# Last normalisation: both parameter rows in matmul banks, two blocks to ScalarE and GpSimd, two through the tensor engine one at a time

## The chip, the cores and the metric

The kernel runs on one core of one Trainium2 chip. The metric is the device time of one execution in microseconds (us), as the median of several runs. The engines are TensorE (PE in the profile), VectorE (DVE), ScalarE (ACT), GpSimd (POOL) and SyncE (SP), which here only issues transfers.

## What is computed

One encoder layer over 1024 tokens of 1024 channels in float32: a mixing sub-layer (convolution and chunked attention), then a grouped mixture of experts, each followed by a layer norm. Only the last step matters here:

```
def layer_norm(x, g, b):
    mu = mean(x); var = mean((x - mu)**2)
    return (x - mu) * rsqrt(var + 1e-5) * g + b
x = layer_norm(ALPHA * x + grouped_moe(x, ...), ln2_g, ln2_b)
```

`ln2_g` and `ln2_b` are rows of 1024 channels, the same for every token.

## The kernel before, in words

Tokens lie on the 128 partitions, in 8 blocks t = 0 to 7 of 128 tokens. The experts run over tiles of 128 gathered tokens (20 or so, the count is read at run time). Each tile's result, times its weight, is added by an indirect transfer into `acc_dram`, whose row has 1024 channels and, as its last element, their sum. The last tile isn't added there: its rows of `acc_dram` are gathered into `rows_l`, the result in the two banks ps 6 and 7 is added by VectorE (`last_rows`), and they are normalised as a ninth block (t = 8, `TT`) and scattered over the output at the very end by GpSimd, which first waits for all eight stores of the output (`f_out`).

The last stage runs over t = 0 to 8. Rows of `acc_dram` come into `xf[:, t]` (eight loads by SyncE, L1434). For each block VectorE makes the negative mean `nmr` (`mean`, L2075); ScalarE squares with that bias and sums (L1846), and takes the root (L1849); VectorE makes (x + nmr) * g (`scale_row`, L2082), then the reciprocal (L2088), and, in `finish`, times rstd plus b (L2094). For blocks 1, 3 and 5 (`ON_PE`), `finish` writes only a diagonal matrix of rstd (L2091); TensorE makes ident x b (L1730) plus diag x rows (L1734) in two banks per block, and ScalarE copies them back (L1853). ScalarE also sums `rows_l` with a copy to `norm_l` (L1844). `g2_b` and `b2_b` hold the two parameter rows on every partition in SBUF, loaded during the experts. Order within an engine is the order in the program; engines wait on semaphores: `f_nm` (mean), `f_sq` (squares), `f_sd` (root), `f_rs` (reciprocal), `f_g` (scaled), `f_ok` (finished), `tot_set` (copied back), `fin_done` (matmuls done), `ln2_in` (parameters loaded).

VectorE's loop is

```
mean(0)
for t in range(TT + 1):
    if t == TT // 2:
        last_rows()
    if t < TT:
        mean(t + 1)
    scale_row(t)
    finish(t)
```

SyncE issues the eight stores of `xf` (L1441) in the order t = 0 to 7, each after a wait for its block; a block that is late holds back those behind it.

On TensorE, ahead of this stage, the last tiles run `up_rows`, `transpose_h(end1)` (four transposes of `hb`, L1652) and `down(end1)` (24 products, L1556 to L1558, with `dn_h`, `dn_l`).

Of the kernel before, what the change touches and what calls it, by code (L numbers as in the profile page):

```python
# [83 lines left out]
def encoder_layer(nc, xT, x, wblk, b_in, dw, dwb, lncg, lncb, relb, b_o, ln1_g, ln1_b,  # L84
# [5 lines left out]
    with ctx:  # L90
# [155 lines left out]
        blk_used = sem("blk_used")  # L246
        zero_ok = sem("zero_ok"); zero_out = sem("zero_out"); init_p = sem("init_p")
        sig_ready = sem("sig_ready"); u_ready = sem("u_ready"); conv_d = sem("conv_d")
# [19 lines left out]
        ln_g = sem("ln_g"); x1_ok = sem("x1_ok")  # L268
        x1_out = sem("x1_out"); acc_out = sem("acc_out"); wr_in = sem("wr_in"); cst_in = sem("cst_in")

# [121 lines left out]
        with nc.Block() as block:  # L392
            @block.sync
            def _(sp):
# [31 lines left out]
                sp.wait_ge(zero_ok, 1)  # L426
                sp.dma_start(acc_dram[SEQ:SEQ + P, :], zeros[:]).then_inc(zero_out, 16)
                for n in range(RING, B_V[0] + RING):
# [41 lines left out]
                for t in range(TT):  # L470
                    if t == TT - 1:
                        sp.wait_ge(wo_done, 2 * TT)
                        moe_parts["load_expert_1"](sp, 0, 2)
                    sp.wait_ge(x1_ok, t + 1)
                    if t == 5:
                        sp.dma_start(upto_t[:], consts[:, C_UPTO:C_WIDTH]).then_inc(cst_in, 16)
                    sp.dma_start(x1_dram[P * t:P * t + P, :], x1[:, t, :]).then_inc(x1_out, 16)
                    sp.dma_start(acc_dram[P * t:P * t + P, 0:D], x1[:, t, :]).then_inc(acc_out, 16)
# [820 lines left out]
def moe(nc, sem, m):  # L1299
# [6 lines left out]
    (x1, x1t, hot_a, hot_b, wr_t, ones, rt_a, rt_b, rank_a, rank_b, slot_i, mh, sums, xgh2, xgl2, hot_0, both, upto_t, val, wide, tc, id0, one_i, init_p, wo_add, gu, dn_h, dn_l, dn_raw, xg, xgh, xgl, hb, hbh, hbl, ys,  # L1306
     xf, g2_b, b2_b, rows_l, norm_l, ys2, diag, squares, x1_tot, w_last, to_last, cst, eps2, st6, mv, rstd, nmr, wgt, ids_i, id_now, to_i, to_now, w_slot, tab, cum_i, ends_i, rows_i, br_b,
     ps, psf, ident) = (m[k] for k in (
         "x1 x1t hot_a hot_b wr_t ones rt_a rt_b rank_a rank_b slot_i mh sums xgh2 xgl2 hot_0 both upto_t val wide tc id0 one_i init_p wo_add gu dn_h dn_l dn_raw xg xgh xgl hb hbh hbl ys "
         "xf g2_b b2_b rows_l norm_l ys2 diag squares x1_tot w_last to_last cst eps2 st6 mv rstd nmr wgt ids_i id_now to_i to_now w_slot tab cum_i ends_i rows_i br_b "  # L1310
         "ps psf ident").split())
    wexp, ln2_g, ln2_b, out, x1_dram, acc_dram = (m[k] for k in "wexp ln2_g ln2_b out x1_dram acc_dram".split())
    row_in, wr_in, cst_in, wo_done, x1_ok, x1_out, acc_out, xres_ok = (
        m[k] for k in "row_in wr_in cst_in wo_done x1_ok x1_out acc_out xres_ok".split())
    gu_in = [sem(f"gu_in{j}") for j in range(4)]; dn_in = sem("dn_in")
# [12 lines left out]
    rows_in = sem("rows_in"); rows_ok = sem("rows_ok"); w_set = sem("w_set"); last_stored = sem("last_stored")  # L1328
    tot_set = sem("tot_set"); fin_done = sem("fin_done"); f_nm = sem("f_nm"); f_sq = sem("f_sq"); f_sd = sem("f_sd")
    f_rs = sem("f_rs"); f_g = sem("f_g"); f_ok = sem("f_ok"); f_out = sem("f_out")  # L1330
# [128 lines left out]
    def pool_part(pool):  # L1459
# [100 lines left out]
    def tensor_part(pe):  # L1560
# [145 lines left out]
        def step(i):  # L1706
# [46 lines left out]
    def scalar_part(act):  # L1753
# [178 lines left out]
    def vector_part(dve):  # L1932
# [137 lines left out]
        def mean(t):  # L2070
            if t < TT:
                dve.wait_ge(row_in[t], 32)
            else:
                dve.wait_ge(rows_ok, 2)
            dve.tensor_scalar(nmr[:, t:t + 1], xf[:, t, D:D + 1] if t < TT else mv[:, t, 0:1], -1.0 / D, None, ALU.mult).then_inc(f_nm, 1)  # L2075

        def scale_row(t):
            dve.wait_ge(f_nm, t + 1)
            if t < TT:

                dve.wait_ge(f_sq, t + 1)
            dve.scalar_tensor_tensor(out=xf[:, t, 0:D] if t < TT else norm_l[:], in0=xf[:, t, 0:D] if t < TT else rows_l[:, 0:D],  # L2082
                                     scalar=nmr[:, t:t + 1], in1=g2_b[:], op0=ALU.add, op1=ALU.mult).then_inc(f_g, 1)

        def finish(t):
            rows = xf[:, t, 0:D] if t < TT else norm_l[:]
            dve.wait_ge(f_sd, t + 1)
            dve.reciprocal(rstd[:, t:t + 1], rstd[:, t:t + 1]).then_inc(f_rs, 1)  # L2088
            dve.wait_ge(f_rs, t + 1)
# [3 lines left out]
            dve.wait_ge(f_g, t + 1)  # L2093
# [68 lines left out]
```

## Time and profile before

| | |
|---|---|
| median of 3 runs | 1140.38 us (1139.57 to 1140.88) |
| the profiled execution's own time | 1142.64 us |
| its span, first to last instruction | 1140.8 us |
| busy share of the span: PE, DVE, ACT, POOL | 96%, 70%, 46%, 21% |
| mean granted TensorE clock | 0.986 of full speed |

The span is what the trace shows; 1.8 us of the profiled execution lie around it. Times in the rows below are microseconds from the span's start. The last normalisation fills 1109 to 1134.

### The profile page before, as it was taken

The numbers are of one execution on the slowest core, as the hardware profiler recorded it, in microseconds if no ns is written. First come the engines' busy times: TensorE is split into PE (matmuls) and PEld (weight loads), VectorE is DVE, ScalarE is ACT, GpSimd is POOL, SyncE is SP. The second block draws the span as 40 slices with busy tenths as digits, with TensorE's granted clock in tenths as the row PEclk, the third lists the DMA queues.
The fourth block names the chain that finished last, engine by engine and source line by source line (L and its number), as shares of the span: only waits on it lengthen the run. The fifth ranks groups of instructions, "written<-read, shape, count | busy, mean of one in ns | idle before, by whom it ended". The sixth has DMA issues, their size and how long they took to land.

```text
span 1140.8 us, 16949 instructions
## 1 busy us (share of the span) xinstructions
PE 1098.7 (96%) x5549; PEld 912.7 (80%) x5550; DVE 801.2 (70%) x1153; ACT 528.8 (46%) x786; POOL 234.9 (21%) x191
## 2 busy tenths in 40 slices
PE   7999999999999999999999999999999999999984
PEld 5888888888978889788888887787888888888762
DVE  5699999935447765566685587797589646548767
ACT  5111111123456755646331134377578545648654
POOL 0000000000046864757100000124122111211220
PEclk9999999999999999999999998899999999999987
DMA  7121233232111010271731326589999876699966
GB/s 263 50 90 55 74 111 94 91 111 93 56 37 43 19 43 1 87 301 38 256 136 60 148 111 250 216 321 361 327 328 383 310 240 189 214 378 326 344 202 239
DMA packets 49797, 199.57 MB, mean 175 GB/s; under 512 B 7248, under 2 KB 7632, under 8 KB 47680
## 3 DMA queue, kind: packets, MB, share of 16 engines
q1 hardware_dynamic: 43536, 176.19, 41.1%
q0 software_dynamic: 6192, 22.49, 8.0%
q8 instruction: 40, 0.66, 0.3%
q14 instruction: 29, 0.24, 0.1%
HBM read 166.21 MB, written 32.52 MB: 174 GB/s over the span
## 4 chain that ended last, share of the span: by engine, by line
PE 84%; DMA 5%; DVE 5%; ACT 2%; POOL 2%; issue 2%; ACTq 0%; DVEq 0%; SPq 0%; POOLq 0%
PE ps L540 16%; PE ps L542 16%; PE ps L541 16%; PE ps L1556 9%; PE ps L1558 9%; PE ps L1557 8%; DMA gu<-in_wexp 3%; PE ps L640 2%; PE ps L626 2%; PE ps L612 2%; PE ps L1625 1%; PE ps L1552 1%; DMA dn_raw<-in_wexp 1%; PE ps L1540 1%; POOL pr L498 1%
## 5 line engine op out<-in xcount | busy, mean ns | idle before, releaser
L540 PE MATMUL ps<-xh,wh 128*128 128x512 f32 x512 | 204.5, 399 | 8.3 <-DVE xl L1024 8.0
L541 PE MATMUL ps<-xl,wh 128*128 128x512 f32 x512 | 200.6, 392 | 0.0
L542 PE MATMUL ps<-xh,wl 128*128 128x512 f32 x512 | 200.4, 391 | 0.0
L498 POOL TENSOR_SCALAR pr<-pr,rinv 128x640 f32<-128x640 f32 (+4 forms) x64 | 94.3, 1486 | 382.4 <-DVE rinv L1148 382.2
L1456 DVE TENSOR_TENSOR gu<-gu (+1 forms) x128 | 148.6, 1220 | 32.7 <-issue 22.3
L1047 DVE SCALAR_TENSOR_TENSOR cv<-u,dw_t,cv 128x1024 f32<-128x1024 f32 x120 | 154.1, 1284 | 3.7
L1450 ACT ACTIVATE gu<-gu (+1 forms) x128 | 124.4, 1048 | 27.2 <-DMA gu<-in_wexp 19.6
L1556 PE MATMUL ps<-gu,xgh 128*128 x336 | 133.2, 397 | 3.5 <-DVE xgl L1930 3.4
L1558 PE MATMUL ps<-gu,xgl 128*128 x336 | 131.2, 390 | 0.0
L1557 PE MATMUL ps<-gu,xgh 128*128 x336 | 130.8, 389 | 0.0
L540 PEld LDWEIGHTS ps<-xh,wh 128*128 128x128 f32 x512 | 96.8, 189 | 31.2 <-issue 12.0
L542 PEld LDWEIGHTS ps<-xh,wl 128*128 128x128 f32 x512 | 96.8, 189 | 20.5
L541 PEld LDWEIGHTS ps<-xl,wh 128*128 128x128 f32 x512 | 97.0, 189 | 19.5 <-issue 0.5
L856 ACT ACTIVATE wh<-raw 128x1024 fp32r<-128x1024 f32 x52 | 54.6, 1058 | 97.4 <-DMA raw<-in_wblk 97.1
L1019 DVE TENSOR_TENSOR wl<-raw,wh 128x1024 fp32r<-128x1024 f32 x39 | 47.6, 1222 | 50.1 <-ACT wh L856 50.1
L2022 DVE TENSOR_TENSOR dn_l<-dn_raw,dn_h 128x1024 fp32r<-128x1024 f32 x60 | 69.6, 1219 | 11.9 <-ACT dn_h L1773 11.0
L1556 PEld LDWEIGHTS ps<-gu,xgh 128*128 128x128 f32 x336 | 63.1, 188 | 17.2 <-issue 4.9
L1558 PEld LDWEIGHTS ps<-gu,xgl 128*128 128x128 f32 x336 | 63.1, 188 | 13.4
L1557 PEld LDWEIGHTS ps<-gu,xgh 128*128 128x128 f32 x336 | 63.2, 188 | 12.5
L1556 PE MATMUL ps<-dn_h,hbh 128*128 128x512 f32 x168 | 68.4, 407 | 1.9 <-DVE hbl L2026 1.9
L1557 PE MATMUL ps<-dn_l,hbh 128*128 128x512 f32 x168 | 66.5, 396 | 0.0
L1558 PE MATMUL ps<-dn_h,hbl 128*128 128x512 f32 x168 | 66.5, 396 | 0.0
(271 smaller groups left out, 2028.4 us busy)
## 6 DMA issues: line engine op xcount, KB each, us to landing
gu<-in_wexp SPq DMA_DIRECT2D x64, 1024.0 KB, 8.9
dn_raw<-in_wexp SPq DMA_DIRECT2D x16, 2048.0 KB
raw<-in_wblk SPq DMA_DIRECT2D x52, 512.0 KB, 4.1
gate_cols<-gst SPq DMA_DIRECT2D x16, 512.0 KB, 5.1
xf<-acc_rows SPq DMA_DIRECT2D x8, 512.5 KB, 7.9
xraw<-in_xT SPq DMA_DIRECT2D x8, 512.0 KB, 7.5
gcm<-gate_cols SPq DMA_DIRECT2D x8, 512.0 KB, 7.0
gam<-gate_cols SPq DMA_DIRECT2D x8, 512.0 KB, 15.6
```

The lines of the kernel that those rows point to most:

```text
L498: pool.tensor_scalar(pr[n % 3][:, h, 0:nt * P], pr[n % 3][:, h, 0:nt * P], rinv[:, n % 3, h:h + 1], None, ALU.mult).then_inc(p_ready, 1)
L540: pe.matmul(o, a_h, b_h, start=first, stop=False)
L541: pe.matmul(o, a_h, b_l, start=False, stop=False)
L542: return pe.matmul(o, a_l, b_h, start=False, stop=last)
L856: act.activation(hi, src, ACT.Copy).then_inc(w_hi, 1)
L1047: dve.scalar_tensor_tensor(out=cv[:, j, :], in0=tap, scalar=w, in1=cv[:, j, :], op0=ALU.mult, op1=ALU.add).then_inc(conv_d, 1)
L1450: eng.activation(gu[:, par, k, 0, :], gu[:, par, k, 1, :].bitcast(F32), ACT.Copy).then_inc(gu_hi, 1)
L1456: eng.tensor_tensor(gu[:, par, k, 1, :], gu[:, par, k, 1, :].bitcast(F32), gu[:, par, k, 0, :], ALU.subtract).then_inc(gu_lo, 1)
L1556: pe.matmul(o, a_h, b_h, start=first, stop=False)
L1557: pe.matmul(o, a_h, b_l, start=False, stop=False)
L1558: return pe.matmul(o, a_l, b_h, start=False, stop=last)
L2022: dve.tensor_tensor(dn_l[:, k, :], dn_raw[:, k, :], dn_h[:, k, :], ALU.subtract).then_inc(dn_lo, 1)
```

## The change

- `norm_rows(0)` and `norm_rows(1)` on TensorE multiply `g2_b` and `b2_b` by the identity into banks 0 and 1, and 2 and 3: before `transpose_h(end1)` and after it. VectorE waits for both after `mean(0)` and reads g and b there.
- Blocks 1 and 2 (`ON_POOL`): VectorE makes nmr * rstd (`shift`), ScalarE x * rstd + shift, GpSimd times g, then plus b.
- Blocks 3 and 5 (`ON_PE`) go through banks 4 and 5, the second after the first was copied back.
- The sum of `rows_l` comes out of `last_rows` itself, and ScalarE's copy to `norm_l` goes.
- Semaphores are merged: `zero_out` into `acc_out`, `cst_in` into `wr_in`, with the counts waited for raised.

```
@@ constants
-    ON_PE = (1, 3, 5)
-    STORED = {t: n for n, t in enumerate(t for t in range(TT + 1) if t not in ON_PE)}
+    ON_PE = (3, 5)
+    ON_POOL = (1, 2)
+    SCALED = {t: n for n, t in enumerate(t for t in range(TT + 1) if t not in ON_POOL)}
+    STORED = {t: n for n, t in enumerate(t for t in SCALED if t not in ON_PE)}
@@ SyncE, order of the stores
             if t in ON_PE:
                 sp.wait_ge(tot_set, 2 + ON_PE.index(t))
+            elif t in ON_POOL:
+                sp.wait_ge(z_done, 2 * ON_POOL.index(t) + 2)
             else:
@@ GpSimd, after the gather of rows_l
+        pool.wait_ge(ln2_in, 32)
+        for n, t in enumerate(ON_POOL):
+            pool.wait_ge(z_ok, n + 1)
+            pool.tensor_tensor(xf[:, t, 0:D], xf[:, t, 0:D], g2_b[:], ALU.mult).then_inc(z_done, 1)
+            pool.wait_ge(z_done, 2 * n + 1)
+            pool.tensor_tensor(xf[:, t, 0:D], xf[:, t, 0:D], b2_b[:], ALU.add).then_inc(z_done, 1)
         pool.wait_ge(f_ok, STORED[TT] + 1)
@@ TensorE
+        def norm_rows(n):
+            rows = (g2_b, b2_b)[n]
+            pe.wait_ge(ln2_in, 32)
+            for h in range(2):
+                last = pe.matmul(ps[:, 2 * n + h, :], ident, rows[:, HALF * h:HALF * h + HALF], start=True, stop=True)
+            last.then_inc(fin_done, 1)
+        norm_rows(0)
         transpose_h(end1)
+        norm_rows(1)
         down(end1, by_row=True)
         for n, t in enumerate(ON_PE):
-            halves_of = [(ps[:, 2 * n + h, :], slice(HALF * h, HALF * h + HALF)) for h in range(2)]
+            if n:
+                pe.wait_ge(tot_set, 1 + n)
             (ident x b, then diag x rows, now both into ps 4 and 5)
@@ ScalarE, in the loop over t, after the root
+            if t - 1 in ON_POOL:
+                n = ON_POOL.index(t - 1)
+                act.wait_ge(f_rs, t + n + 1)
+                act.activation(xf[:, t - 1, 0:D], xf[:, t - 1, 0:D], ACT.Identity, scale=rstd[:, t - 1:t],
+                               bias=shift[:, t - 1:t]).then_inc(z_ok, 1)
@@ ScalarE, before t == TT - 2
-                act.activation(norm_l[:], rows_l[:, 0:D], ACT.Copy, accum_out=mv[:, TT, 0:1]).then_inc(rows_ok, 1)
@@ VectorE
-                                     scalar=nmr[:, t:t + 1], in1=g2_b[:], op0=ALU.add, op1=ALU.mult).then_inc(f_g, 1)
+                                     scalar=nmr[:, t:t + 1], in1=psf[:, 0:D], op0=ALU.add, op1=ALU.mult).then_inc(f_g, 1)
+            if t in ON_POOL:
+                dve.tensor_scalar(shift[:, t:t + 1], nmr[:, t:t + 1], rstd[:, t:t + 1], None, ALU.mult).then_inc(f_rs, 1)
+                return
-            dve.scalar_tensor_tensor(out=rows, in0=rows, scalar=rstd[:, t:t + 1], in1=b2_b[:],
+            dve.scalar_tensor_tensor(out=rows, in0=rows, scalar=rstd[:, t:t + 1], in1=psf[:, D:2 * D],
@@ VectorE, last_rows
-                                     op0=ALU.mult, op1=ALU.add).then_inc(rows_ok, 1)
+                                     op0=ALU.mult, op1=ALU.add, accum_out=mv[:, TT, 0:1]).then_inc(rows_ok, 1)
@@ VectorE, the loop
-        dve.wait_ge(ln2_in, 32)
         mean(0)
+        dve.wait_ge(fin_done, 2)
         for t in range(TT + 1):
             if t == TT // 2:
                 last_rows()
             if t < TT:
                 mean(t + 1)
-            scale_row(t)
+            if t not in ON_POOL:
+                scale_row(t)
             finish(t)
```

## Rows read from the trace of the kernel before

**Rows 1.** The chain of waits, its end: start us, us, what

```profile
1130.27 1.30 DVE xf L2094
...
1131.59 2.62 DMA out_rows<-xf
1134.21 0.03 POOLq L1528
...
1135.14 1.02 POOL out_rows L1529
```

**Rows 2.** The timeline of VectorE: start us, us, engine, line, operation, names

```profile
1109.05 0.22 DVE L2075 TENSOR_SCALAR nmr<-xf 128x1 f32<-128x1 f32 x2
...
1119.14 1.28 DVE L2101 SCALAR_TENSOR_TENSOR rows_l<-ps,w_last,rows_l 128x1024 f32<-128x1024 f32 x1
1120.34 0.14 DVE L2075 TENSOR_SCALAR nmr<-xf 128x1 f32<-128x1 f32 x1
...
1132.67 0.16 DVE L2088 RECIPROCAL rstd<-rstd 128x1 f32<-128x1 f32 x1
1132.86 1.28 DVE L2094 SCALAR_TENSOR_TENSOR norm_l<-norm_l,rstd,b_b 128x1024 f32<-128x1024 f32 x1
```

**Rows 3.** The timeline of ScalarE in the same stage

```profile
1114.65 0.30 ACT L1849 ACTIVATE rstd<-mv,eps 128x1 f32<-128x1 f32 x1
...
1120.03 1.14 ACT L1846 ACTIVATE squares<-xf,nmr 128x1024 f32<-128x1024 f32 x1
...
1121.29 0.29 ACT L1849 ACTIVATE rstd<-mv,eps 128x1 f32<-128x1 f32 x1
1121.49 1.13 ACT L1846 ACTIVATE squares<-xf,nmr 128x1024 f32<-128x1024 f32 x1
```

**Rows 4.** Groups by shape from 1098 on: busy us, mean ns | idle before

```profile
L2082 DVE SCALAR_TENSOR_TENSOR xf<-xf,nmr,g_b 128x1024 f32<-128x1024 f32 x8 | 10.2, 1280 | 2.7 <-ACT squares L1846 2.7
...
L1844 ACT ACTIVATE norm_l<-rows_l 128x1024 f32<-128x1024 f32 x1 | 1.0, 1044 | 0.0
...
L2091 DVE TENSOR_SCALAR diag<-ident_t,rstd 128x128 f32<-128x128 f32 x3 | 0.9, 287 | 0.1
```

**Rows 5.** Groups by shape over the whole span, ScalarE and VectorE

```profile
L914 ACT ACTIVATE cv<-cv,cpar 128x1024 f32<-128x1024 f32 x4 | 4.6, 1234 | 0.0
```

```profile
L1139 DVE DVE_READ_ACCUMULATOR2_ANT nmx<- 128x1 f32 x62 | 5.1, 83 | 0.0
```

**Rows 6.** Groups by shape of GpSimd over the whole span

```profile
L504 POOL TENSOR_TENSOR wl<-raw,wh 128x1024 fp32r<-128x1024 f32 x13 | 31.2, 2397 | 6.5 <-ACT wh L856 6.5
```

**Rows 7.** The timeline of GpSimd (once ScalarE, its producer) at three places

```profile
383.56 0.20 POOL L512 MEMSET bias<- 64x128 f32 x1
383.82 0.20 POOL L514 MEMSET bias<- 64x128 f32 x1
```

```profile
464.36 1.06 ACT L953 ACTIVATE uoh<-cv 128x1024 fp32r<-128x1024 f32 x1
```

```profile
465.51 2.37 POOL L520 TENSOR_TENSOR uol<-cv,uoh 128x1024 fp32r<-128x1024 f32 x1 [0.19 <-ACT uoh L953]
```

```profile
535.97 7.13 POOL L534 TENSOR_TENSOR al<-attn,ah 128x1024 fp32r<-128x1024 f32 x3
```

**Rows 8.** The timeline of VectorE beside the last of these

```profile
539.42 0.61 DVE L1163 TENSOR_TENSOR attn<-ps,attn 64x128 f32<-64x128 f32 x2
```

**Rows 9.** SyncE's issues, and the stretches with transfers: us, busy by engine, PEclk, DMA share, GB/s

```profile
1120.16 0.81 SPq L1441 DMA_DIRECT2D out_rows<-xf  x2
```

```profile
1121.00:1122.00 1.00, 1.00 (x4) 0.46 (x3) 0.64 (x1) 0.97 (x4) 0.00 (x0) 1.00 1.03 414
1122.00:1123.00 1.00, 1.00 (x4) 0.48 (x3) 0.96 (x3) 0.97 (x4) 0.00 (x0) 1.00 0.99 401
1123.00:1124.00 1.00, 1.00 (x3) 0.19 (x1) 1.00 (x2) 1.00 (x3) 0.00 (x0) 1.00 0.59 229
```

**Rows 10.** The timeline of TensorE around the last transposes

```profile
1104.67 0.66 PE L1652 MATMUL ps<-ident_t,hb 128*128 128x128 f32 x4 [3.00 <-DVE hb L2038]
1107.19 0.79 PE L1556 MATMUL ps<-dn_h,hbh 128*128 128x512 f32 x1 [1.86 <-DVE hbl L2026]
...
1118.91 1.88 PE L1730 MATMUL ps<-b_b,ident_t 128*128 128x512 f32 x4
```

**Rows 11.** One line's instructions: the loads of xf, and VectorE's whole-row scaling

```profile
L1434 SPq DMA_DIRECT2D xf<-acc_rows x8: 326/438/592, 1104.3 to 1107.8; - x8
...
DMA to landing us min/median/max: 3.3/7.9/11.2
```

```profile
L1044 DVE TENSOR_SCALAR cv<-u,dw_t,cpar x4: 806/808/816, 39.8 to 184.6; 128x1024 f32<-128x1024 f32 x4
```

**Rows 12.** Table loads of ScalarE over the whole span, groups by shape

```profile
L1839 ACT ACT_TABLE_LOAD x1 | 1.3, 1283 | 0.0
```

More of the change, by code:

```diff
@@ L212, in encoder_layer @@
         nmr = tiny("nmr", [P, TT + 1])
+        shift = tiny("shift", [P, TT])
         wgt = tiny("wgt", [P, 2, TT])
@@ L246, in encoder_layer @@
         blk_used = sem("blk_used")
-        zero_ok = sem("zero_ok"); zero_out = sem("zero_out"); init_p = sem("init_p")
+        zero_ok = sem("zero_ok"); init_p = sem("init_p")
         sig_ready = sem("sig_ready"); u_ready = sem("u_ready"); conv_d = sem("conv_d")
@@ L268, in encoder_layer @@
         ln_g = sem("ln_g"); x1_ok = sem("x1_ok")
-        x1_out = sem("x1_out"); acc_out = sem("acc_out"); wr_in = sem("wr_in"); cst_in = sem("cst_in")
+        x1_out = sem("x1_out"); acc_out = sem("acc_out"); wr_in = sem("wr_in");
         def wait_used(eng, n):
@@ L426, in _ @@
                 sp.wait_ge(zero_ok, 1)
-                sp.dma_start(acc_dram[SEQ:SEQ + P, :], zeros[:]).then_inc(zero_out, 16)
+                sp.dma_start(acc_dram[SEQ:SEQ + P, :], zeros[:]).then_inc(acc_out, 16)
                 for n in range(RING, B_V[0] + RING):
@@ L475, in _ @@
                     if t == 5:
-                        sp.dma_start(upto_t[:], consts[:, C_UPTO:C_WIDTH]).then_inc(cst_in, 16)
+                        sp.dma_start(upto_t[:], consts[:, C_UPTO:C_WIDTH]).then_inc(wr_in, 16)
                     sp.dma_start(x1_dram[P * t:P * t + P, :], x1[:, t, :]).then_inc(x1_out, 16)
@@ L1306, in moe @@
     (x1, x1t, hot_a, hot_b, wr_t, ones, rt_a, rt_b, rank_a, rank_b, slot_i, mh, sums, xgh2, xgl2, hot_0, both, upto_t, val, wide, tc, id0, one_i, init_p, wo_add, gu, dn_h, dn_l, dn_raw, xg, xgh, xgl, hb, hbh, hbl, ys,
-     xf, g2_b, b2_b, rows_l, norm_l, ys2, diag, squares, x1_tot, w_last, to_last, cst, eps2, st6, mv, rstd, nmr, wgt, ids_i, id_now, to_i, to_now, w_slot, tab, cum_i, ends_i, rows_i, br_b,
+     xf, g2_b, b2_b, rows_l, norm_l, ys2, diag, squares, x1_tot, w_last, to_last, cst, eps2, st6, mv, rstd, nmr, shift, wgt, ids_i, id_now, to_i, to_now, w_slot, tab, cum_i, ends_i, rows_i, br_b,
      ps, psf, ident) = (m[k] for k in (
          "x1 x1t hot_a hot_b wr_t ones rt_a rt_b rank_a rank_b slot_i mh sums xgh2 xgl2 hot_0 both upto_t val wide tc id0 one_i init_p wo_add gu dn_h dn_l dn_raw xg xgh xgl hb hbh hbl ys "
-         "xf g2_b b2_b rows_l norm_l ys2 diag squares x1_tot w_last to_last cst eps2 st6 mv rstd nmr wgt ids_i id_now to_i to_now w_slot tab cum_i ends_i rows_i br_b "
+         "xf g2_b b2_b rows_l norm_l ys2 diag squares x1_tot w_last to_last cst eps2 st6 mv rstd nmr shift wgt ids_i id_now to_i to_now w_slot tab cum_i ends_i rows_i br_b "
          "ps psf ident").split())
     wexp, ln2_g, ln2_b, out, x1_dram, acc_dram = (m[k] for k in "wexp ln2_g ln2_b out x1_dram acc_dram".split())
-    row_in, wr_in, cst_in, wo_done, x1_ok, x1_out, acc_out, xres_ok = (
-        m[k] for k in "row_in wr_in cst_in wo_done x1_ok x1_out acc_out xres_ok".split())
+    row_in, wr_in, wo_done, x1_ok, x1_out, acc_out, xres_ok = (
+        m[k] for k in "row_in wr_in wo_done x1_ok x1_out acc_out xres_ok".split())
     gu_in = [sem(f"gu_in{j}") for j in range(4)]; dn_in = sem("dn_in")
@@ L1328, in moe @@
     rows_in = sem("rows_in"); rows_ok = sem("rows_ok"); w_set = sem("w_set"); last_stored = sem("last_stored")
-    tot_set = sem("tot_set"); fin_done = sem("fin_done"); f_nm = sem("f_nm"); f_sq = sem("f_sq"); f_sd = sem("f_sd")
+    tot_set = sem("tot_set"); fin_done = sem("fin_done"); z_ok = sem("z_ok"); z_done = sem("z_done"); f_nm = sem("f_nm"); f_sq = sem("f_sq"); f_sd = sem("f_sd")
     f_rs = sem("f_rs"); f_g = sem("f_g"); f_ok = sem("f_ok"); f_out = sem("f_out")
@@ L1409, in sync_part @@
         sp.wait_ge(x1_out, 16 * TT)
-        sp.wait_ge(acc_out, 16 * TT)
+        sp.wait_ge(acc_out, 16 * TT + 16)
         sp.wait_ge(xt_r, TT)
@@ L1470, in pool_part @@
         pool.wait_ge(x1_out, 16 * TT)
-        pool.wait_ge(acc_out, 16 * TT)
+        pool.wait_ge(acc_out, 16 * TT + 16)
         pool.wait_ge(xt_r, TT)
@@ L1511, in pool_part @@
         step(1, False)
-        pool.wait_ge(acc_out, 16 * TT + 16)
+        pool.wait_ge(acc_out, 16 * TT + 32)
         step(2)
@@ L1721, in tensor_part @@
         up_rows(NE - 1, bass.ds(par, 1), range(KC // 2, KC))
+        norm_rows(0)
         transpose_h(end1)
+        norm_rows(1)
         down(end1, by_row=True)
-        pe.wait_ge(ln2_in, 32)
         for n, t in enumerate(ON_PE):
-            halves_of = [(ps[:, 2 * n + h, :], slice(HALF * h, HALF * h + HALF)) for h in range(2)]
-            for o, c in halves_of:
-                pe.matmul(o, ident, b2_b[:, c], start=True, stop=False)
-            pe.wait_ge(f_g, t + 1)
+            if n:
+                pe.wait_ge(tot_set, 1 + n)
+            for h in range(2):
+                pe.matmul(ps[:, 4 + h, :], ident, b2_b[:, HALF * h:HALF * h + HALF], start=True, stop=False)
+            pe.wait_ge(f_g, SCALED[t] + 1)
             pe.wait_ge(diag_ok, n + 1)
-            for o, c in halves_of:
-                last = pe.matmul(o, diag[:, n, :], xf[:, t, c], start=False, stop=True)
+            for h in range(2):
+                last = pe.matmul(ps[:, 4 + h, :], diag[:, n, :], xf[:, t, HALF * h:HALF * h + HALF], start=False, stop=True)
             last.then_inc(fin_done, 1)
@@ L1840, in scalar_part @@
         for t in range(TT + 1):
-            if t == TT - 2:
-                act.wait_ge(rows_ok, 1)
-                act.activation(norm_l[:], rows_l[:, 0:D], ACT.Copy, accum_out=mv[:, TT, 0:1]).then_inc(rows_ok, 1)
             act.wait_ge(f_nm, t + 1)
@@ L1849, in scalar_part @@
             act.activation(rstd[:, t:t + 1], mv[:, t, 1:2], ACT.Sqrt, scale=1.0 / D, bias=eps2[:]).then_inc(f_sd, 1)
+            if t - 1 in ON_POOL:
[3 more added lines that the diff above has]
+                               bias=shift[:, t - 1:t]).then_inc(z_ok, 1)
             if t - 2 in ON_PE:
                 n = ON_PE.index(t - 2)
-                act.wait_ge(fin_done, n + 1)
-                act.activation(xf[:, t - 2, 0:D], psf[:, D * n:D * n + D], ACT.Copy).then_inc(tot_set, 1)
+                act.wait_ge(fin_done, n + 3)
+                act.activation(xf[:, t - 2, 0:D], psf[:, 4 * HALF:6 * HALF], ACT.Copy).then_inc(tot_set, 1)
     V = nc.vector
@@ L1958, in vector_part @@
         ee = wide[:, 0:NE * NE].rearrange("p (a b) -> p a b", b=NE)
-        dve.wait_ge(cst_in, 16)
+        dve.wait_ge(wr_in, 64)
         link(V.tensor_tensor(ee, upto, nt.unsqueeze(1).broadcast_to([P, NE, NE]), ALU.mult))
@@ L2073, in mean @@
             else:
-                dve.wait_ge(rows_ok, 2)
+                dve.wait_ge(rows_ok, 1)
             dve.tensor_scalar(nmr[:, t:t + 1], xf[:, t, D:D + 1] if t < TT else mv[:, t, 0:1], -1.0 / D, None, ALU.mult).then_inc(f_nm, 1)
@@ L2088, in finish @@
             dve.reciprocal(rstd[:, t:t + 1], rstd[:, t:t + 1]).then_inc(f_rs, 1)
-            dve.wait_ge(f_rs, t + 1)
+            shifts = sum(p < t for p in ON_POOL)
+            dve.wait_ge(f_rs, t + shifts + 1)
+            if t in ON_POOL:
+                dve.tensor_scalar(shift[:, t:t + 1], nmr[:, t:t + 1], rstd[:, t:t + 1], None, ALU.mult).then_inc(f_rs, 1)
+                return
             if t in ON_PE:
@@ L2092, in finish @@
                 return
-            dve.wait_ge(f_g, t + 1)
-            dve.scalar_tensor_tensor(out=rows, in0=rows, scalar=rstd[:, t:t + 1], in1=b2_b[:],
+            dve.wait_ge(f_g, SCALED[t] + 1)
+            dve.scalar_tensor_tensor(out=rows, in0=rows, scalar=rstd[:, t:t + 1], in1=psf[:, D:2 * D],
                                      op0=ALU.mult, op1=ALU.add).then_inc(f_ok, 1)
```

## The prediction

> **What bounds the kernel now.** I began at the end of the chain of waits [rows 1]. Behind the final scatter by GpSimd (L1529) stands the last of eight stores, landed at 1134.21 after its issue at 1131.59, and ahead of that VectorE's finish of block 7. The ninth block's finish ends at 1134.14 [rows 2], so two things release the scatter within 0.1 us of each other. From 1134.21 to the span's end at 1140.8 is a tail of 6.6 us that the change leaves alone. Then the timeline of VectorE [rows 2]: from its first mean at 1109.05 it does a row operation of 1.28 us behind the other, 1.20 from start to start (1119.14 to 1120.34). By groups, eight L2082 with only 2.7 us of waiting before them [rows 4]: this stage is bound by VectorE. Before 1109 nothing of weight is edited. TensorE's 96% of the span doesn't bear on this stage.
>
> **What is removed from VectorE.** Blocks 1 and 2 lose L2082 twice and block 2 its L2094: three row operations, 3.6 us at 1.20. Block 1 trades its diagonal (about 0.2) for a `shift`, block 2 gains a `shift`; such small ones cost 0.07 to 0.2. That is not the gain, because VectorE now runs ahead of ScalarE and waits.
>
> **ScalarE, step by step.** Until the root of block 2 at 1114.65 [rows 3] nothing moves: squares 2 waits for VectorE's mean 2, which still stands behind block 0's finish. Root to next operation takes 0.20 (1121.29 to 1121.49), squares to root 1.26 (1120.03 to 1121.29) [rows 3]. So Identity of block 1 starts at 1114.85. Its price isn't shown: a copy from SBUF takes 1.04 [rows 4], an activation with scale and bias by partition 1.23 [rows 5]; I take 1.14, as squares with a bias takes. It ends at 1115.99; squares 3 starts at 1115.9, its sum is there at 1117.15. VectorE has been through mean 2, reciprocal and shift 1, mean 3, reciprocal and shift 2, mean 4 by 1115.5 and stands until 1117.2: 1.7 us of the 3.6 are lost. Identity of block 2 ends at 1118.5. Means 3 and 4 come at about 1113.7 and 1115.4 and need their loads: eight landings from 1104.3 + 3.3 = 1107.6 to 1107.8 + 11.2 = 1119.0 [rows 11], 1.6 apart if even, so 1112.5 and 1114.1. Covered, by some 1.2 us.
>
> **VectorE from 1117.2.** Scale 3, last rows, scale and finish 4, scale 5, scale and finish 6, scale and finish 7, scale 8 are ten at 1.20 = 12.0; six reciprocals at 0.19 (1132.67 to 1132.86 [rows 2]) = 1.14; two diagonals at 0.21; four means at 0.07 = 0.28; the accumulator read of the new sum 0.08 [rows 5]. Together 13.9: finish 8 starts at 1131.1 and ends at 1132.4, 1.7 before its old 1134.14. Finish 7 starts 2.6 earlier, at 1128.55, and ends at 1129.8. That g and b come from the banks I cost at nothing: L2101 reads a bank and takes 1.28 [rows 2], L2082 without one 1280 ns [rows 4]. Squares 5 to 8 and the two copies fit beside this (each ScalarE step follows its mean at once), and the dropped L1844 only widens the room.
>
> **TensorE.** `norm_rows(0)` is two products of 0.43 us (1.88 for four, with drain [rows 10]), in a gap of 3.00 ahead of the transposes; `norm_rows(1)`, 0.9, in one of 1.86 behind them [rows 10]. At half the clock the second would take 1.7, still inside. Both are done before 1109.2, when VectorE asks. Without that cover `down(end1)` would be later by up to 1.7, and behind it only `last_rows` waits, at 1118.8, over 3 us after its end. The products of blocks 3 and 5 end by 1121 and 1126.5, before ScalarE comes to copy at 1121.8 and about 1126. Diagonals cost the tensor engine no more than before. Merged semaphores: the transfers counted in are long landed; nothing.
>
> **GpSimd, the new path.** Its nearest row operation, two SBUF inputs of 128x1024, takes 2.40 us [rows 6]. It starts 0.09 after ScalarE's end (464.36 + 1.06 = 465.42 to 465.51) [rows 7], and a wait on its own last operation costs 0.06 (383.76 to 383.82) [rows 7]. From 1116.08: 4 x 2.40 + 3 x 0.06 = 9.78, so block 2 is ready at 1125.86. Block 1 is ready at 1120.9, about as early as it was stored before (1120.16 [rows 9]).
>
> **Stores, where the gain goes.** SyncE's queue is in order. Block 2 was stored right behind block 1 before; now at 1125.9, and 3 and 4, ready by 1123, stand behind it, while the transfers idle from 1123. Then six stores go in a row. Two, issued at 1120.16, moved 1.04 MB in 1121.0 to 1123.6 [rows 9]: 0.85 from issue to first data, 1.29 for each. A lone store lands in 2.62 [rows 1], so 0.48 come behind the data. 1125.9 + 0.85 + 6 x 1.29 + 0.48 = 1134.97. Block 7, issued at 1129.85, alone would land at 1132.5, but is last in this row; all data of blocks 2 to 6 take until 1133.2. So `f_out` releases the scatter at 1134.97 against 1134.21: 0.76 later, although VectorE is done 1.7 earlier.
>
> **The sum.** Span 1140.8 + 0.8 = 1141.6; the execution's own time 1142.64 + 0.8 = 1143.4. The runs' median lies 2.26 under that execution, so 1140.38 + 0.76 = 1141.1 us. I count as no change what is within 0.2%, 2.3 us, about what a measurement here can tell.
>
> **Bounds.** GpSimd's operation: from 1.28 (VectorE's pace) to 2.40. Break-even with the old 1134.21 is at (1125.1 - 1116.08 - 0.18) / 4 = 2.2 us; below 1.75 VectorE's end decides and the gain is its full 1.7. Identity at 1.04 or 1.23 shifts block 2 by 0.1 either way. A further bound: if Identity weren't in the table that holds the root, each use would cost two loads of 1.28 [rows 12]; no row shows Identity beside the root. That would put z of block 1 at 1117.3 and that of block 2 at 1122.3, block 2 ready at 1127.2 (+1.3), and VectorE over 2.6 later: a loss of about 2. The Trainium skill (ScalarE: Activation LUTs) says that cheap functions, identity among them, are in every set; by that, no load comes, which no run here shows yet.
>
> **Rival A, VectorE's diagonal blocked by GpSimd.** A whole-row scaling by L1044 takes 808 ns for 1024 elements [rows 11], the two-tensor form 1280 [rows 4]: VectorE's scaling runs at two elements a step. If it uses the path that GpSimd reads by, it waits out a GpSimd operation. Diagonal 3 comes at 1118.6, just as GpSimd starts its second operation, and would stand until 1120.95: VectorE is 2.3 later throughout, finish 8 ends at 1134.7, block 7 is issued at 1132.1, and goes right behind the other stores, landing at 1135.2 if GpSimd lost 0.3 too: +1.0, 1141.4. If the small means are caught too (mean 5 for 1.3), finish 7 ends at 1133.6, its store lands at 1136.3: +2.1, 1142.5. For it: nothing in the trace of before runs such a scaling beside GpSimd. Against: two-tensor operations with one SBUF input do run beside it at full speed (L1163 at 0.30 each while GpSimd does three in 7.13 [rows 7, 8]). The Trainium skill (SBUF — State Buffer, "Who interferes with whom") says just this: a `tensor_scalar` in a 2-port mode and a GpSimd operation lock each other out for a whole instruction, while a VectorE operation with one SBUF input doesn't contend; by it the row operations are free and the diagonals wait.
>
> **Rival B, GpSimd quick enough.** Operations under 1.75 us: stores catch up, and VectorE's end sets it: -1.7, 1138.7. Against: 13 operations at a mean of 2.40 [rows 6].
>
> **Rival C, the other side.** VectorE and GpSimd take turns, row by row, even with g and b in banks. Place: 1116 to 1126. Each of four GpSimd operations stands behind a row operation of 1.28: block 2 is ready 5.1 later and the six stores land at 1140.1: +5.9, 1146.3. It decides from GpSimd operations of 2.8 us on (+2.3 at the end). Against: rows 8.
>
> **How the numbers follow.** Forecast 0.50; rival A 0.24 (a fourth of it over the bound of slower, with late stores added); rival B or another gain 0.12, half of it past 0.2%; rival C, or the table loads, 0.14, most of it slower. Slower: 0.06 + 0.11 + 0.02 of the forecast = 0.19; faster 0.06; same 0.75. The forecast alone: 1140.3 to 1142.0 (spread of the runs 0.6, GpSimd's bound). The range reaches to rival B's 1138.7, less the spread, and past A's 1142.5 by as much: 1138.7 to 1143.2; C's far end is left out.
>
> **What would show it.** SyncE's stores: 1 at about 1121, 2, 3, 4 together at about 1125.9, and the transfers busy without a gap to 1134.5. VectorE: idle of 1.7 before L2082 of block 3 on ScalarE's squares, end of `norm_l` at 1132.4. The wait of the scatter: on the store, no longer level with VectorE. A diagonal of 2 us, or an idle stretch before it, would show rival A; GpSimd rows over 2.8, C; under 1.75, B. The prediction is wrong if VectorE's end or the stores' row stands elsewhere, or if `norm_rows` holds up `down(end1)`.

## The result, and the profile after

The changed kernel takes 1144.82 us (median of 6, 1143.19 to 1145.57) against 1140.63 (6 runs): a ratio of 1.0029, 95% interval 1.0018 to 1.0041. It is slower, by about 0.3%, and above the range I gave (to 1143.2); a second timing, below, gives 1.0020 (1.0008 to 1.0032). I had forecast 1141.1 and no change, and gave slower 0.19.

Single executions of one kernel spread over 3 to 10 us here, more than most effects below, and three slow ones (1234.84, 1382.9 and 2226.04 us) are left out of the ratios. So beside the ratios I read each profile by the length of the last stage: from the start of VectorE's first mean to the moment at which the scatter's wait ends (`POOLq` in the chain). Before it is 1134.21 - 1109.05 = 25.16 [rows 1, 2]. After, 1136.14 - 1109.36 = 26.78. Each such length is that of one execution. Here is the timeline of VectorE after, with the rows that answer to [rows 2] and the diagonals that answer to L2091 in [rows 4]:

```profile
1109.36 0.21 DVE L2095 TENSOR_SCALAR nmr<-xf 128x1 f32<-128x1 f32 x2
...
1115.28 0.16 DVE L2108 RECIPROCAL rstd<-rstd 128x1 f32<-128x1 f32 x1 [1.25 <-ACT rstd L1864]
...
1117.61 1.28 DVE L2102 SCALAR_TENSOR_TENSOR xf<-xf,nmr,ps 128x1024 f32<-128x1024 f32 x1 [1.86 <-ACT squares L1861]
1118.81 0.15 DVE L2108 RECIPROCAL rstd<-rstd 128x1 f32<-128x1 f32 x1
1119.00 2.39 DVE L2115 TENSOR_SCALAR diag<-ident_t,rstd 128x128 f32<-128x128 f32 x1
1121.31 1.27 DVE L2125 SCALAR_TENSOR_TENSOR rows_l<-ps,w_last,rows_l 128x1024 f32<-128x1024 f32 x1
...
1126.59 0.29 DVE L2115 TENSOR_SCALAR diag<-ident_t,rstd 128x128 f32<-128x128 f32 x1
...
1133.91 1.28 DVE L2118 SCALAR_TENSOR_TENSOR norm_l<-norm_l,rstd,ps 128x1024 f32<-128x1024 f32 x1
```

Up to 1119 this is what I worked out, 0.3 to 0.5 later. Then the diagonal of block 3 stands for 2.39 us; the second, with GpSimd idle, takes 0.29. GpSimd after, which answers to [rows 6, 7]:

```profile
1116.54 2.35 POOL L1534 TENSOR_TENSOR xf<-xf,g_b 128x1024 f32<-128x1024 f32 x1 [10.35 <-ACT xf L1868]
1118.97 2.34 POOL L1536 TENSOR_TENSOR xf<-xf,b_b 128x1024 f32<-128x1024 f32 x1
1121.27 2.00 POOL L1534 TENSOR_TENSOR xf<-xf,g_b 128x1024 f32<-128x1024 f32 x1
1123.34 2.00 POOL L1536 TENSOR_TENSOR xf<-xf,b_b 128x1024 f32<-128x1024 f32 x1
```

The diagonal begins just behind the second row's start (1118.97) and ends with it: rival A's place, to 0.1 us when both are counted from the first mean. TensorE after, answering to [rows 10]. One call of `matmul` on 512 columns shows here as two instructions, so one block's ident x b, or its diagonal products, is a line of x4:

```profile
1113.07 1.88 PE L1750 MATMUL ps<-b_b,ident_t 128*128 128x512 f32 x4
1121.54 3.47 PE L1754 MATMUL ps<-xf,diag 128*128 128x512 f32 x4 [6.58 <-DVE diag L2115]
1126.12 1.98 PE L1750 MATMUL ps<-b_b,ident_t 128*128 128x512 f32 x4 [1.11 <-ACT xf L1873]
1127.94 1.88 PE L1754 MATMUL ps<-xf,diag 128*128 128x512 f32 x4
```

and its granted clock by stretches (us, PE busy, PEclk, DMA share, GB/s):

```profile
1113.00:1115.00 2.00, 1.95 (x5) 1.00 1.03 418
1115.00:1118.00 3.00, 0.00 (x0) 0.96 1.02 321
1118.00:1121.00 3.00, 0.00 (x0) 0.50 0.46 187
1121.50:1125.00 3.50, 3.46 (x4) 0.56 0.37 150
```

```profile
1131.33 1.29 DVE xf L2118
...
1132.64 3.51 DMA out_rows<-xf
1136.14 0.03 POOLq L1539
...
1137.07 1.03 POOL out_rows L1540
```

Block 5 is stored at 1130.91 and 6 behind it, so block 7's store takes 3.51 to land, not the 2.62 of a lone one: the data of 5 and 6 go ahead of it. From issue to the first data 0.85, three at 1.29, 0.48 behind: 1130.91 + 5.20 = 1136.11.

### The profile page after: what moved, and what is told of

Its sections match the earlier page's. It is cut to its first block, busy times and chain, and to the rows that moved or that the text cites. A ratio compares the mean times of both kernels' runs of the same rounds, so it can differ in the third digit from the quotient of the medians.

```text
span 1142.8 us, 16948 instructions
## 1 busy us (share of the span) xinstructions
PE 1098.5 (96%) x5549; PEld 912.3 (80%) x5550; DVE 799.9 (70%) x1152; ACT 529.4 (46%) x785; POOL 243.9 (21%) x195
## 4 chain that ended last, share of the span: by engine, by line
PE 83%; DMA 5%; DVE 5%; ACT 2%; POOL 2%; issue 2%; DVEq 0%; ACTq 0%; SPq 0%; POOLq 0%
PE ps L541 16%; PE ps L542 15%; PE ps L543 15%; PE ps L1567 8%; PE ps L1569 8%; PE ps L1568 8%; DMA gu<-in_wexp 3%; PE ps L641 2%; PE ps L627 2%; PE ps L613 2%; PE ps L1636 1%; PE ps L1563 1%; DMA dn_raw<-in_wexp 1%; PE ps L1551 1%; PE ps L1663 1%
## 5 line engine op out<-in xcount | busy, mean ns | idle before, releaser
L1461 DVE TENSOR_TENSOR gu<-gu (+1 forms) x128 | 148.6, 1221 | 32.7 <-issue 22.3
```

The source lines that it names most:

```text
L1461: eng.tensor_tensor(gu[:, par, k, 1, :], gu[:, par, k, 1, :].bitcast(F32), gu[:, par, k, 0, :], ALU.subtract).then_inc(gu_lo, 1)
```

## The experiments

Two faults stand in that trace: the diagonal that waits, and blocks 3 and 5 on a slow tensor engine. The stage lengths of these profiles, first mean to release, in us, with the timed ratios to before and their intervals:

| kernel | first mean, release | stage | ratio |
|---|---|---|---|
| before | 1109.05, 1134.21 | 25.16 | |
| e1 merged semaphores only | 1108.13, 1132.33 | 24.20 | 1.0006 (0.9993 to 1.0020) |
| after | 1109.36, 1136.14 | 26.78 | 1.0029 (1.0018 to 1.0041) |
| e12 after, again | 1108.32, 1135.40 | 27.08 | 1.0020 (1.0008 to 1.0032) |
| e2 diagonal without the wait | 1107.17, 1134.29 | 27.12 | 1.0027 (1.0012 to 1.0041) |
| e3 stores reordered | 1108.83, 1135.82 | 26.99 | 1.0024 (1.0010 to 1.0039) |
| e4 e2 and e3 | 1110.88, 1137.77 | 26.89 | 1.0019 (1.0005 to 1.0033) |
| e5 e2, TensorE kept busy | 1109.33, 1134.63 | 25.30 | 1.0004 (0.9993 to 1.0015) |
| e13 TensorE kept busy only | 1106.96, 1134.27 | 27.31 | 1.0032 (1.0020 to 1.0044) |
| e6 e2, block 5 in banks 6, 7 | 1107.07, 1132.85 | 25.78 | 1.0007 (0.9992 to 1.0022) |
| e7 g and b read from SBUF | 1109.17, 1139.18 | 30.01 | 1.0042 (1.0024 to 1.0059) |
| e8 e5, means two ahead, stores | 1106.32, 1129.28 | 22.96 | 0.9991 (0.9980 to 1.0003) |
| e10 e8, xf 1026 apart | 1107.73, 1131.61 | 23.88 | 0.9991 (0.9979 to 1.0004) |
| e11 before, means two ahead | 1107.85, 1131.98 | 24.13 | 1.0001 (0.9989 to 1.0012) |

**e1, the merged semaphores alone.** The first medians lie 4.2 us apart, the stages 1.6. Is there a loss elsewhere?

```
-  ... zeros[:]).then_inc(zero_out, 16)
+  ... zeros[:]).then_inc(acc_out, 16)
-  ... .then_inc(cst_in, 16)
+  ... .then_inc(wr_in, 16)      (and the counts waited for raised)
```

> The kernel before with nothing of the change but the merged semaphores (zero_out into acc_out, cst_in into wr_in). The medians of before and after lie 4.2 us apart, the two profiled executions only 2.0 (1142.64 to 1144.6). Theory: all of the loss is in the last stage, and this kernel is level with before, ratio 1.000 within 0.001. Rival: the merged semaphores or the shifted code cost some 2 us ahead of 1109, around the routing; then 1142.6 or so, ratio 1.002.

1.0006: the merging costs nothing that shows, though the interval ends just at the rival's 1.0020. Its profile gives the old stage a second time, at 24.20, not 25.16. The profile that I predicted from had a stage 1 us longer: its `down(end1)` ran at half clock to 1113 and block 1 was copied back 10.1 us after the first mean, against 8.75 in e1.

**e12, the change again.**

> The changed kernel as it is, timed again with more runs of both. The stage is 1.6 to 2.6 us longer than before by the profiles (26.8 against 25.2 and 24.2 from the first mean to the release), while the first medians lie 4.2 apart. Theory: the rest of the 4.2 is the spread of few runs, and the ratio comes to 1.0015 to 1.0025. Rival (something outside the stage costs 1.5 us more): 1.003 or above.

1.0020, stage 27.08. The stage is 1.6 to 2.9 us longer than before (26.78 to 27.08 against 25.16 and 24.20), 0.14 to 0.25% of 1140.6, and both ratios' intervals hold 1.0018 to 1.0025. The ratio is where the theory had it. The rest of the first 4.2 us is the spread of six runs, as far as can be told.

**e2, the diagonal without the wait.**

```
-  dve.tensor_scalar(diag[:, ON_PE.index(t), :], ident, rstd[:, t:t + 1], None, ALU.mult).then_inc(diag_ok, 1)
+  dve.scalar_tensor_tensor(out=diag[:, ON_PE.index(t), :], in0=ident, scalar=rstd[:, t:t + 1],
+                           in1=psf[:, 0:P], op0=ALU.mult, op1=ALU.bypass).then_inc(diag_ok, 1)
```

> The changed kernel with the diagonal made by a two-tensor operation whose second input is a bank (bypassed), so that VectorE takes one element a step and only one input from SBUF. Theory (the diagonal waits out a GpSimd operation): the 2.39 us row becomes some 0.35, VectorE is 2.1 earlier from there on, TensorE's products of block 3 come sooner, and block 2's late end with the six stores behind it sets the end: 1125.4 + 0.85 + 6 x 1.29 + 0.48 = 1134.4 against 1136.14 after, so 1.7 us faster than the change, ratio to before about 1.0022. Rival (the diagonal isn't blocked by GpSimd, but slow for another reason, for instance the clock of TensorE or a late load): it stays over 1 us and the time does not move.

VectorE and TensorE of e2:

```profile
1116.81 0.35 DVE L2115 SCALAR_TENSOR_TENSOR diag<-ident_t,rstd,ps 128x128 f32<-128x128 f32 x1
```

```profile
1117.31 3.75 PE L1754 MATMUL ps<-xf,diag 128*128 128x512 f32 x4 [4.52 <-DVE diag L2115]
1122.17 3.78 PE L1750 MATMUL ps<-b_b,ident_t 128*128 128x512 f32 x4 [1.11 <-ACT xf L1873]
```

The theory of the wait holds: the same product in a form that takes one element a step beside the same GpSimd row (1116.78 to 1119.15) takes 0.35. The expected gain doesn't come: 27.12. The 2.1 us won on VectorE are lost on TensorE, where the low clock now lasts through block 5's ident x b too (3.78), and block 5 is copied back at 1128.01, 20.8 after the first mean, against 1129.86 - 1109.36 = 20.5 in the change.

**e3 and e4, the order of the stores.**

```
-        for t in range(TT):
+        for t in (0, 1, 3, 4, 2, 5, 6, 7):
```

> The changed kernel with SyncE's stores in the order 0, 1, 3, 4, 2, 5, 6, 7. Theory (the diagonal's wait binds; block 3 is copied back only at 1126.1): no gain, as 3 and 4 aren't ready before 2; within 0.3 us of the change. Rival (the order of the stores binds as I forecast): a gain of 1 us or more.

> Both: the diagonal without the wait, and stores in the order 0, 1, 3, 4, 2, 5, 6, 7. Theory: 3 and 4 are ready by 1123.3 and go while GpSimd works on 2; the last store is issued at about 1130.1 and the ninth block ends at 1132.8, so the scatter is released at about 1132.9, 1.5 us earlier than with the diagonal alone and 3.2 than the change: a ratio to before of about 1.001 or lower. Rival (the stores were never the limit): the same as the diagonal alone.

e3: 26.99, as the theory had it. e4: 26.89 where 23.5 was expected (1132.9 - 1109.36), and 1.0019 where 1.001 or lower was: that expectation still took TensorE as quick. In both the last row of stores starts with block 5, not with block 2. So the stores behind block 2, my forecast's bound, bind in none of these.

**e5, TensorE kept busy.** Six products of 128x512 that nobody reads:

```
+            if n == 0:
+                for _ in range(4):
+                    pe.matmul(ps[:, 4, :], ident, b2_b[:, 0:HALF], start=True, stop=True)
             if n:
+                pe.wait_ge(rows_ok, 1)
+                for _ in range(2):
+                    pe.matmul(ps[:, 6, :], ident, b2_b[:, 0:HALF], start=True, stop=True)
                 pe.wait_ge(tot_set, 1 + n)
```

> The kernel of e2 (diagonal without the wait) with products added on TensorE whose result nobody reads: four of 128x512 ahead of block 3's ident x b, two between block 3 and block 5. In e2 the products of block 3 took 3.75 us for four rows and block 5's ident x b 3.78, at a granted clock of half, and block 5 was copied back only 20.8 us after the first mean. Theory (with the diagonal's wait gone, the tensor engine's half clock binds, block by block): blocks 3 and 5 take 1.9 for each four rows, block 5 is copied at 17.6 after the first mean, and the scatter is released 25.1 after it, against 27.15 in e2 and 26.8 after; about 2 us off the stage, ratio to before about 1.001. Rival (GpSimd's late block 2 binds, as forecast): the stage stays at 27 from the first mean to the release.

TensorE by stretches in e5, and the end of its chain:

```profile
1113.00:1118.30 5.30, 5.30 (x13) 1.00 1.01 368
1119.40:1121.40 2.00, 1.93 (x5) 1.00 0.28 115
1121.40:1127.00 5.60, 5.56 (x13) 1.00 0.38 153
```

```profile
1130.19 4.44 DMA out_rows<-xf
1134.63 0.03 POOLq L1539
```

Full clock throughout, block 5 copied back from 1127.01, 17.7 after the first mean (17.6 expected), and the stage 25.30 (25.1 expected). Now the bound of my forecast is the one at the end: block 7's store takes 4.44 to land, since six stores go in a row from block 2 on. GpSimd ends at 1125.34, and 1125.34 + 0.85 + 7.74 + 0.48 = 1134.4. Even with both faults gone the change is only level with before (1.0004, interval to 1.0015).

**e13, the fourth corner.** The same products with the diagonal as in the change.

> The changed kernel with only the products that keep TensorE at its full clock (four ahead of block 3, two between 3 and 5); the diagonal of block 3 still waits. It fills the fourth corner: release after the first mean was 26.8 to 27.1 with both faults, 27.1 without the diagonal's wait, 25.3 with neither. If the half clock alone binds, this one comes to 25.3 to 25.8; if either fault alone is enough for the whole loss, it stays at 26.5 or more.

The timeline of VectorE and of TensorE in e13, the diagonal and block 3's products:

```profile
1116.60 2.39 DVE L2121 TENSOR_SCALAR diag<-ident_t,rstd 128x128 f32<-128x128 f32 x1
```

```profile
1119.14 3.65 PE L1760 MATMUL ps<-xf,diag 128*128 128x512 f32 x4 [3.13 <-DVE diag L2121]
```

27.31. But the corner is not the one I wanted: the waiting diagonal leaves TensorE idle for 3.13 us and the clock falls after all (0.54 from 1119 to 1121), so both faults are in this trace; up to 0.5 of its length is the two added products between the blocks, which here stand behind the late block 3. Shown is that each remedy alone gives nothing and both together give 1.5 to 1.8 us: 26.8 to 27.1 without either, 27.12, 27.31, and 25.30. The half clock is enough for the whole loss without the diagonal's wait (e2). That the wait would be enough at full clock isn't shown. An estimate from these rows says no: e5's block 5 is stored 18.7 after the first mean (17.7 and 1.05 for the copy), the wait adds 2.39 - 0.35 = 2.04, three stores from there take 5.20, together about 26.0.

**e6, block 5 through banks 6 and 7.**

```
             if n:
-                pe.wait_ge(tot_set, 1 + n)
+                pe.wait_ge(rows_ok, 1)
             (outputs to ps 4 + 2 * n + h, copied back from there)
```

> The kernel of e2 with block 5 through banks 6 and 7 (free after last_rows) instead of waiting until block 3 was copied back. Theory of the half clock: only the wait of 1.1 us between the two goes, the clock stays low, so the stage gets at most 1 us shorter than e2 (26.2 or more from the first mean to the release). Rival (it is the one-at-a-time order that binds): over 2 us shorter.

25.78, 1.3 shorter than e2: between the two expectations. The clock was also low for a shorter time (block 5's ident x b took 2.71, not 3.78), so this doesn't divide the loss between order and clock; it shows that, with the diagonal's wait gone, giving up the order gets back most of what the full clock gets back in e5.

**e7, g and b from SBUF.**

```
-                                     scalar=nmr[:, t:t + 1], in1=psf[:, 0:D], ...
+                                     scalar=nmr[:, t:t + 1], in1=g2_b[:], ...      (and b2_b in finish)
```

> The changed kernel with VectorE reading g and b from SBUF, as before; norm_rows still runs. If a VectorE operation with two inputs from SBUF and a GpSimd one shut each other out, the two take turns: GpSimd's four rows end 2 us or more later than after's 1125.34 - 1109.36 = 16.0 from the first mean, and VectorE's rows beside them show 2 us and more instead of 1.28. The whole is 2 to 6 us slower than the change. If the banks do nothing, rows and times stay as after.

The timeline of e7, VectorE's scaling of block 3 and GpSimd's two additions:

```profile
1117.43 2.35 DVE L2102 SCALAR_TENSOR_TENSOR xf<-xf,nmr,g_b 128x1024 f32<-128x1024 f32 x1 [1.86 <-ACT squares L1861]
```

```profile
1118.77 3.20 POOL L1536 TENSOR_TENSOR xf<-xf,b_b 128x1024 f32<-128x1024 f32 x1
...
1124.01 2.86 POOL L1536 TENSOR_TENSOR xf<-xf,b_b 128x1024 f32<-128x1024 f32 x1
```

VectorE's row waits out GpSimd's and GpSimd's wait out VectorE's; the stage is 3 us longer than the change's. The timed ratio is only 0.0013 above the change's, some 1.5 us and under the 2 to 6 expected, with overlapping intervals. GpSimd ends 17.7 after the first mean, 1.7 later than the 16.0 in the change, a little under the 2 I expected. The banks do what they are there for: with one input from SBUF all row operations stay at 1.28 beside GpSimd.

**e8, e10, e11, toward a better one.**

```
         mean(0)
+        mean(1)
         for t in range(TT + 1):
-            if t < TT:
-                mean(t + 1)
             scale_row(t)      (not for the blocks of GpSimd)
+            if t < TT - 1:
+                mean(t + 2)
             finish(t)
```

> e5 with two things more: VectorE makes the mean two blocks ahead (between scale and finish), and the stores go in the order 0, 1, 3, 4, 2, 5, 6, 7. VectorE's idle of 1.25 and 1.86 us for ScalarE comes from the mean of block 2 standing behind block 0's finish. Theory: ScalarE begins squares 2 1.2 earlier and all behind it moves by about 1 us; release at 23 from the first mean, against 25.2 and 24.2 in the two profiles with the old stage: level with or up to 1.5 us faster than before. Rival (the loads of xf bind): the mean of block 4 waits for its load, and nothing is gained over e5.

> e8 (diagonal without the wait, warm TensorE, mean two ahead, stores 0, 1, 3, 4, 2, 5, 6, 7) with the rows of xf 1026 apart. If GpSimd's alignment is worth 0.7 us on block 2 and its store was not last, the release stays at 22.3 to 23.0 from the first mean (22.96 in e8). Ratio to before 0.998 to 0.9995.

> The kernel before with only VectorE's mean two blocks ahead. Theory (the old stage is VectorE's row operations, 16 at 1.20, with 2.7 us of waits on ScalarE): the first wait of 1.1 goes, the release comes 23 to 24 from the first mean (25.2 and 24.2 before), so half or more of e10's gain needs none of the change. Rival (the mean isn't what ScalarE lacks): 24.2 or more.

e8's stage is 22.96, 1.2 to 2.2 shorter than before, and its mean of block 4 waits 1.11 us for its load; e10's 23.88, longer than the 22.3 to 23.0 expected: TensorE was at half clock just ahead of it (`norm_rows(1)` 3.44 us), which may be why but wasn't tried. Both time at 0.9991 with intervals that hold 1. e11's stage is 24.13, at the edge between its theory and its rival, and its time level: before, the early mean mostly moves the wait (ScalarE waits 1.11 us for the mean of block 2 in e1 and 0.91 for that of block 3 in e11). A version that beats both kernels beyond what can be measured isn't shown; e8 and e10 are faster than the change (their intervals end at 1.0003 and 1.0004, its two begin at 1.0018 and 1.0008).

**e9 and e14, the two prices of a GpSimd row.**

```
-        xf = at("xf", [P, TT, D + 1], F32, 128)
+        xf = at("xf", [P, TT, D + 2], F32, 128)                      (e9)
+        xf = at("xf", [P, TT, D + 4], F32, 128)[:, :, 2:D + 4]       (e14)
```

> The changed kernel with the rows of xf 1026 elements apart instead of 1025. In all traces of the change GpSimd's two rows on block 1 take 2.35 us and the two on block 2 2.00. Theory (the start of block 1 is 4 bytes off a multiple of 8, that of block 2 isn't): with every block on a multiple of 8 all four take 2.00, and block 2 is ready 0.7 us earlier. Rival (the loads of xf, which run until 1119, or the neighbour's work slow the first two): 2.35, 2.35, 2.00, 2.00 as before.

> The changed kernel with every block of xf starting 8 bytes past a multiple of 16 (rows 4112 bytes apart, first at 8). In the change block 1 starts at 4 modulo 16 and took 2.35 us a row on GpSimd, block 2 at 8 and took 2.00; with a pitch of 4104 block 1 started at 8 and took 2.00, block 2 at 0 and took 2.36. Theory (8 modulo 16 is the quick start): all four take 2.00. Rival (something in the order or in the other operand): one pair stays at 2.35.

e9, GpSimd:

```profile
1114.49 1.99 POOL L1534 TENSOR_TENSOR xf<-xf,g_b 128x1024 f32<-128x1024 f32 x1 [9.12 <-ACT xf L1868]
1116.56 2.00 POOL L1536 TENSOR_TENSOR xf<-xf,b_b 128x1024 f32<-128x1024 f32 x1
1118.52 2.36 POOL L1534 TENSOR_TENSOR xf<-xf,g_b 128x1024 f32<-128x1024 f32 x1
1120.96 2.35 POOL L1536 TENSOR_TENSOR xf<-xf,b_b 128x1024 f32<-128x1024 f32 x1
```

My first theory fell: with every block on a multiple of 8 the prices changed places. Block 1 now starts at 8 modulo 16, block 2 at 0. In e14, where all start at 8 modulo 16, all four take 2.00 (first and last of them):

```profile
1116.71 1.99 POOL L1534 TENSOR_TENSOR xf<-xf,g_b 128x1024 f32<-128x1024 f32 x1 [9.19 <-ACT xf L1868]
...
1122.81 2.00 POOL L1536 TENSOR_TENSOR xf<-xf,b_b 128x1024 f32<-128x1024 f32 x1
```

So it is the address, neither the order nor the loads; why it is so wasn't tried. Both are single executions, without a ratio. In both the diagonal waited 1.69 instead of 2.39, since GpSimd's second row ended sooner, and both stages are 26.37.

## Why the prediction was wrong, point by point

**What bounds.** Right in kind: before, VectorE and the last store end nearly together, and the tail behind the release stayed (6.6 before, 6.7 after). But the baseline was one profile with a stage 1 us longer than in e1. That this execution lay 2.26 us over the runs' median stood in my own text, and I carried it across as a constant instead of asking which part of it lay in the stage. The forecast was a release 0.76 later; against the same profile it came 26.78 - 25.16 = 1.62 later, against e1's 2.58.

**ScalarE.** Right: Identity 1.23 (1.14 taken, 1.04 to 1.23 given), VectorE's wait ahead of block 3 1.86 (1.7 forecast). No table load came with Identity, as the Trainium skill (ScalarE: Activation LUTs, "Table sets: the hidden batching unit") has it; the trace agrees, root and Identity alternate at 1114.95 and 1115.16.

**VectorE.** The sum of 13.9 from scale 3 to finish 8 was right without the diagonal: in e5 it is 1131.46 - 1117.58 = 13.9. With it, 1133.91 - 1117.61 = 16.3. "Two diagonals at 0.21" is the first term that failed: 2.39 for one. That was rival A's mechanism, given 0.24, and the Trainium skill's rule (SBUF — State Buffer, "Who interferes with whom") holds in both halves: a `tensor_scalar` in a 2-port mode waits out a GpSimd operation (2.39 against 0.35 in e2), a row with one SBUF input does not, one with two does (2.35 in e7). The small means weren't caught: 0.14 and 0.15 beside GpSimd in the change. Rival A also had VectorE's times: it put the issue of block 7's store 23.05 after the first mean, and it came at 23.28. Its price was still short, a release at 26.15 where 26.78 was measured, for it took TensorE as free.

**TensorE, the step that failed.** "The products of blocks 3 and 5 end by 1121 and 1126.5, before ScalarE comes to copy at 1121.8 and about 1126." From the first mean the two ends are 11.95 and 17.45. Measured, they came at 1125.01 and 1129.82, 15.65 and 20.46 after it, and ScalarE waited for both. The forecast had two terms at nothing: the diagonal's wait, which it left to rival A, and the half clock, which it gave no reason to rule out. Taking block 1 away and running two blocks one behind the other leaves TensorE idle for 6.58 us, 2.1 of them the diagonal's wait, and the granted clock was 0.50 when its work came; in e2, with 4.52 idle, it was the same. I priced half clock only for `norm_rows`. Since block 5 comes last in that order, its delay goes right onto the stores: issued 21.55 after the first mean. With both terms gone, in e5, the forecast's times nearly hold, 12.10 and 17.65:

```profile
1119.47 1.96 PE L1760 MATMUL ps<-xf,diag 128*128 128x512 f32 x4 [1.14 <-DVE diag L2121]
...
1123.16 1.98 PE L1756 MATMUL ps<-b_b,ident_t 128*128 128x512 f32 x4
1125.02 1.96 PE L1760 MATMUL ps<-xf,diag 128*128 128x512 f32 x4
```

I also misread x4 [rows 10] as four calls: it is two, so `norm_rows` costs 1.88 and not 0.9, and 3.44 at half clock (e10) and not 1.7. That did no harm in the change, where `down(end1)` starts 1.85 ahead of the first mean and in the trace of before 1.86.

**Stores, where the gain goes.** The mechanism was right and not the bound. It shows in e5, where the release is 25.30 after the first mean; my figures gave 1134.97 - 1109.05 = 25.9, with GpSimd at 2.40 where it measured 2.35 and 2.00. The mean of its four operations, 2.17, is just under my break-even of 2.2, and e5's 25.30 is level with the 25.16 of before.

**Rivals B and C.** B's condition (rows under 1.75) wasn't met. C's mechanism showed only with both inputs in SBUF (e7).

**Not settled.** How much of the first 4.2 us is the stage: 1.6 to 2.9 by the profiles, the rest within the runs' spread. Order against clock for blocks 3 and 5 (e6 moved both). And the diagonal's wait with TensorE at full clock, which no run has.

## What to carry to other kernels

Moving work off the busiest engine pays only as far as the engines that take it are quick at that moment: ask how long they will have stood idle by then, and read their clock in the stretch where they'll be asked. Where GpSimd computes, look at each VectorE instruction beside it, small ones too: one `tensor_scalar` of 128 columns cost 2.4 us, and a bank as second input avoided it. Two faults can each look harmless when they are removed one at a time, since one can hide or bring back the other; try both remedies together, and look in the trace whether each did what it was for.

## What the runs showed of the hardware that I had not expected

A GpSimd `tensor_tensor` of 128x1024 float32 took 2.00 us where its rows started at 8 modulo 16 bytes from the start of `xf`'s place in SBUF, and 2.34 to 2.36 at 0 or 4 (change, e9, e14), for multiply and add alike. And a diagonal that waits for GpSimd undid the products that were to keep TensorE at full clock: an idle of 3.13 us stood ahead of the half clock in e13, where e5, with 1.14 us, kept full clock.
